# An S5 drive two half units earlier in a hybrid decoder trunk: VectorE's branch work, scores and S5 outputs in another order

## The reference

```
h    = x * (1 + scale) + shift
proj = h @ w_in                       # 2048 -> 6144, in 12 parts of 512 channels
A: y_a = a_b * causal_conv3(a_c * a_x) * silu(a_g)
B: y_b = dilated window attention(q, k, v), 8 heads of 64, three dilations mixed * silu(b_g)
C: y_c = RG-LRU(causal_conv4(c_x)) * silu(c_g)      # two gate products, one scan over time
D: y_d = S5(d_u) * silu(d_g)          # complex diagonal scan, y = Re(C x) + D u, gelu, GLU
y    = concat(y_a, y_b, y_c, y_d) @ w_out
x    = LayerNorm(alpha * x + (1 + gate) * y)
```

## Time and profile before

| | |
|---|---|
| median of three runs | 1848.13 us (1841.9 to 1850.42) |
| profiled execution, its own time | 1842.14 us |
| span of its profile | 1840.3 us |
| mean granted TensorE clock | 0.957 of full speed |
| TensorE busy (matmuls) | 1669.3 us, 91% |
| VectorE busy | 1249.6 us, 68% |
| ScalarE busy | 774.4 us, 42% |
| POOL busy | 233.1 us, 13% |

### The profile page before, as it was taken

How to read it: one execution, slowest core, us unless ns; L and a number is a source line. 1 busy time by engine, 2 the same in 40 slices (tenths; PEclk the granted TensorE clock), 3 DMA queues, 4 the chain that set the end, 5 groups by cost and what they waited for, 6 DMA issues and landing times.

```text
span 1840.3 us, 23052 instructions
## 1 busy us (share of the span) xinstructions
PE 1669.3 (91%) x7527; PEld 1294.5 (70%) x7527; DVE 1249.6 (68%) x2361; ACT 774.4 (42%) x1014; POOL 233.1 (13%) x281
## 2 busy tenths in 40 slices
PE   2339999999999999799998999999999999979995
PEld 1337778777777877568876777777877777748884
DVE  5885984895698489556673587398378468643658
ACT  2135444554544454421226554554555455432220
POOL 2242111111111111000004111111111111100000
PEclk9559999999999999899998999999999999989998
DMA  7999879978988988747656888978988887727422
GB/s 261 375 328 255 216 188 234 237 197 217 231 204 207 244 211 208 194 148 236 199 183 187 191 192 196 218 186 196 203 201 200 186 203 190 183 80 257 137 92 103
DMA packets 322945, 376.07 MB, mean 204 GB/s; under 512 B 27064, under 2 KB 224032, under 8 KB 319784
## 3 DMA queue, kind: packets, MB, share of 16 engines
q1 hardware_dynamic: 294632, 272.36, 46.0%
q0 software_dynamic: 28224, 102.77, 31.0%
HBM read 261.81 MB, written 10.51 MB: 148 GB/s over the span
## 4 chain that ended last, share of the span: by engine, by line
PE 58%; DVE 30%; issue 6%; DMA 3%; ACT 1%; SPq 1%; DVEq 0%; POOL 0%; ACTq 0%; POOLq 0%
PE bank L944 12%; PE bank L951 11%; PE bank L945 11%; DVE work L1285 9%; PE bank L987 6%; PE bank L984 6%; PE bank L985 6%; DVE ada_acc L1293 3%; DVE work L1293 3%; DVE work L1147 2%; DVE work L1146 2%; PE bank L963 2%; DVE carry L1293 2%; DVE y_t L1293 1%; DVE work L1289 1%
## 5 line engine op out<-in xcount | busy, mean ns | idle before, releaser
L944 PE MATMUL bank<-op_hi,w_hi 128*128 128x512 f32 x1536 | 617.5, 402 | 0.0
L945 PE MATMUL bank<-op_lo,w_hi 128*128 128x512 f32 x1536 | 602.8, 392 | 0.0
L951 PE MATMUL bank<-op_hi,w_lo 128*128 128x512 f32 x1536 | 379.9, 389 | 4.3 <-DMA w_lo<-raw 4.3
L598 ACT ACTIVATE w_hi<-raw 128x1024 fp32r<-128x1024 f32 x196 | 207.8, 1060 | 397.7 <-PE bank L945 315.1
L944 PEld LDWEIGHTS bank<-op_hi,w_hi 128*128 128x128 f32 x1536 | 290.7, 189 | 88.6 <-issue 21.3
L951 PEld LDWEIGHTS bank<-op_hi,w_lo 128*128 128x128 f32 x1536 | 288.0, 188 | 65.5 <-DMA w_lo<-raw 5.8
L945 PEld LDWEIGHTS bank<-op_lo,w_hi 128*128 128x128 f32 x1536 | 290.7, 189 | 60.1 <-issue 1.9
L550 POOL DMA_DIRECT2D w_lo<-raw x196 | 170.7, 871 | 1077.5 <-ACT w_lo L601 1058.4
L601 ACT ACTIVATE w_lo<-raw 128x1024 fp32r<-128x1024 f32 x196 | 207.2, 1057 | 111.6 <-PE bank L951 111.6
L1293 DVE SCALAR_TENSOR_TENSOR ada_acc<-ada_in,cond,ada_acc 128x512 f32<-128x512 f32 (+1 forms) x234 | 181.4, 775 | 82.3 <-DMA ada_in<-in_w_ada 60.8
L984 PE MATMUL bank<-w_hi,op_hi 128*128 128x512 f32 x480 | 188.2, 392 | 0.0
(11 more groups left out here) (226 smaller groups left out, 1600.8 us busy)
## 6 DMA issues: line engine op xcount, KB each, us to landing
w_lo<-raw POOLq DMA_DIRECT2D x196, 512.0 KB, 5.0
raw<-in_w_in SPq DMA_DIRECT2D x192, 512.0 KB, 4.3
ada_in<-in_w_ada SPq DMA_DIRECT2D x256, 256.0 KB, 4.5
raw<-in_w_out SPq DMA_DIRECT2D x64, 512.0 KB, 4.2
raw<-in_w_ada SPq DMA_DIRECT2D x27, 512.0 KB, 7.0
ada_in<-in_w_ada SPq DMA_DIRECT2D x18, 512.0 KB, 7.1
rot<-in_w_ada SPq DMA_DIRECT2D x10, 512.0 KB, 7.0
bias_t<-in_w_ada SPq DMA_DIRECT2D x9, 512.0 KB, 7.0
```

The source lines that it names most:

```text
L598: act.activation(w_hi[:, n % NHL, :], raw[:, n % NRAW, :], ACT.Copy).then_inc(s.hi_done.sem, 1)
L944: pe.matmul(o, w_hi[:, n % NHL, w], op_hi[:, k, :], start=k == 0, stop=False)
L945: mm = pe.matmul(o, w_hi[:, n % NHL, w], op_lo[:, k, :], start=False, stop=False)
L951: mm = pe.matmul(o, w_lo[:, n % NHL, w], op_hi[:, k, :], start=False, stop=k == KT - 1)
```

## The change

It reorders work and adds or removes none. On TensorE `s5_turn` goes from behind half unit 3 to behind 2, the drives from 5, 7, 10, 13 to 3, 5, 8, 12, `s5_outputs` from 19 to 18, and `scores(2)` and `scores(3)` from 12, 13 to 11, 12. On ScalarE `rotation()` is done behind `split_hi(4)` instead of behind the copy of c_x at 5. On VectorE the LRU's conv goes behind `s5_in(0)`, `s5_in(1)` ahead of the LRU, the score maxima behind later S5 work, `s5_in(3)` ahead of `normalise`, the pieces' calls 11 and 12 elsewhere, and A's conv ahead of D's output. SyncE's and POOL's programs are the same.

```diff
@@ -684,10 +684,11 @@
                             for h in range(2):
                                 swapped = act.activation(u_swap[64 * h:64 * h + 64, :], ps[64 - 64 * h:128 - 64 * h, :], ACT.Copy)
                             swapped.then_inc(free.sem, 1)
+                        if n == 4:
+                            rotation()
                         if n == 5:
                             act.wait_ge(s.step_end.sem, s.step_end.at(0, ct))
                             copy("c_x", xp[:, 3:3 + S])
-                            rotation()
                         if n == 7:
                             copy("q", q_t, HD ** -0.5)
                         if n == 8:
@@ -918,12 +919,12 @@
                     def put(n, part, *args):
                         between[n].append(lambda: part(*args))
 
-                    put(3, s5_turn)
+                    put(2, s5_turn)
                     put(6, lru_gates)
-                    for q, at in enumerate((5, 7, 10, 13)):
+                    for q, at in enumerate((3, 5, 8, 12)):
                         put(at, s5_drive, q)
-                    put(19, s5_outputs)
-                    for t, at in enumerate((9, 10, 12, 13)):
+                    put(18, s5_outputs)
+                    for t, at in enumerate((9, 10, 11, 12)):
                         put(at, scores, t)
                     put(11, v_turn)
                     for g, (at_turn, at_weigh) in enumerate(((16, 18), (18, 20), (20, 22))):
@@ -1107,13 +1108,6 @@
                 ada(2, 1)
                 ada(2, 1)
 
-                unit_copied(dve, s, "c_x", ct)
-                own(ts(xc, xp[:, 3:3 + S], col("conv_c", 12), MUL, col("conv_c_b"), ADD), s.own)
-                for k in (2, 1):
-                    own(stt(xc, xp[:, k:k + S], col("conv_c", 4 * k), xc, MUL, ADD), s.own)
-                own(stt(xc, xp[:, 0:S], col("conv_c"), xc, MUL, ADD), s.xc_done)
-                ada(2, 1)
-
                 w_re, w_im, t_ = (v.rearrange("p (a b) -> p a b", a=4) for v in s5_s[0:3])
                 states = state_tiles(ct)
 
@@ -1193,10 +1187,17 @@
 
                 dve.wait_ge(x_io.sem, 16 * (1 + (ST if l else 0)))
                 s5_in(0)
+                unit_copied(dve, s, "c_x", ct)
+                own(ts(xc, xp[:, 3:3 + S], col("conv_c", 12), MUL, col("conv_c_b"), ADD), s.own)
+                for k in (2, 1):
+                    own(stt(xc, xp[:, k:k + S], col("conv_c", 4 * k), xc, MUL, ADD), s.own)
+                own(stt(xc, xp[:, 0:S], col("conv_c"), xc, MUL, ADD), s.xc_done)
+                ada(2, 1)
                 s5_scan(0)
                 ada(2, 1)
                 s5_out(0)
                 ada(2, 1)
+                s5_in(1)
 
                 dve.wait_ge(s.from_act.sem, s.from_act.at(2, ct))
                 own(ts(lru_s[0], lru_s[0], 1.0, ADD), s.own)
@@ -1207,30 +1208,38 @@
                 own(tt(lru_s[1], lru_s[1], lru_s[2], MUL), s.own)
                 own(dve.tensor_tensor_scan(xc, lru_s[0], lru_s[1], 0.0, MUL, ADD), s.own)
                 ada(2, 1)
-                score_max(0)
-                s5_in(1)
                 s5_scan(1)
                 ada(2, 1)
-                score_max(1)
+                score_max(0)
                 s5_out(1)
                 ada(2, 1)
-                score_max(2)
+                score_max(1)
                 s5_in(2)
                 ada(2, 1)
+                score_max(2)
+                s5_scan(2)
                 score_max(3)
-                s5_scan(2)
+                s5_out(2)
                 ada(2, 1)
-                s5_out(2)
+                s5_in(3)
+                ada(2, 1)
                 normalise(0)
-                ada(2, 1)
                 normalise(1)
                 own(silu2(0, "c_g", gx[:, 0, :]), s.own)
                 own(stt(y_out(2), xc, 0.5, gx[:, 0, :], MUL, MUL), s.gate_used[0])
-                s5_in(3)
+                ada(2, 1)
                 s5_scan(3)
-                ada(2, 1)
                 s5_out(3)
                 own(silu2(1, "d_g", silu_d[:, bass.ds(ct, 1), :].rearrange("p o t -> p (o t)")), s.gate_used[1])
+                ada(2, 1)
+
+                unit_copied(dve, s, "a_x", ct)
+                v = va[:, 2:2 + S]
+                own(tt(v, v, ax, MUL), s.own)
+                cv = s5_s[1]
+                own(ts(cv, v, col("conv_a", 8), MUL), s.own)
+                own(stt(cv, va[:, 1:1 + S], col("conv_a", 4), cv, MUL, ADD), s.own)
+                own(stt(cv, va[:, 0:S], col("conv_a"), cv, MUL, ADD), s.own)
                 ada(2, 1)
 
                 y = s5_s[0]
@@ -1241,15 +1250,6 @@
                 own(tt(gel, s5_s[2], y, MUL), s.to_act)
                 ada(2, 1)
 
-                unit_copied(dve, s, "a_x", ct)
-                v = va[:, 2:2 + S]
-                own(tt(v, v, ax, MUL), s.own)
-                cv = s5_s[1]
-                own(ts(cv, v, col("conv_a", 8), MUL), s.own)
-                own(stt(cv, va[:, 1:1 + S], col("conv_a", 4), cv, MUL, ADD), s.own)
-                own(stt(cv, va[:, 0:S], col("conv_a"), cv, MUL, ADD), s.own)
-
-                ada(2, 1)
                 own(silu2(0, "b_g", gx[:, 0, :]), s.own)
                 dve.wait_ge(s.pv_done.sem, s.pv_done.at(2 * ST, ct))
                 own(stt(y_out(1), bank[7][:, :], 0.5, gx[:, 0, :], MUL, MUL), s.free[7])
```

More of the change, by code:

```diff
@@ L1228, in branch_loop @@
                 own(stt(y_out(2), xc, 0.5, gx[:, 0, :], MUL, MUL), s.gate_used[0])
-                s5_in(3)
+                ada(2, 1)
                 s5_scan(3)
-                ada(2, 1)
                 s5_out(3)
                 own(silu2(1, "d_g", silu_d[:, bass.ds(ct, 1), :].rearrange("p o t -> p (o t)")), s.gate_used[1])
-                ada(2, 1)
-                y = s5_s[0]
-                dve.wait_ge(s.c_done.sem, s.c_done.at(SQ, ct))
-                own(stt(y, u_d, col("s5_d"), bank[4][:, :], MUL, ADD), s.free[4])
-                own(tt(s5_s[2], y, y, MUL), s.own)
-                own(ts(s5_s[2], s5_s[2], 0.044715, MUL, 1.0, ADD), s.own)
-                own(tt(gel, s5_s[2], y, MUL), s.to_act)
                 ada(2, 1)
@@ L1250, in branch_loop @@
                 own(stt(cv, va[:, 0:S], col("conv_a"), cv, MUL, ADD), s.own)
+                ada(2, 1)
+                y = s5_s[0]
+                dve.wait_ge(s.c_done.sem, s.c_done.at(SQ, ct))
+                own(stt(y, u_d, col("s5_d"), bank[4][:, :], MUL, ADD), s.free[4])
+                own(tt(s5_s[2], y, y, MUL), s.own)
+                own(ts(s5_s[2], s5_s[2], 0.044715, MUL, 1.0, ADD), s.own)
+                own(tt(gel, s5_s[2], y, MUL), s.to_act)
                 ada(2, 1)
```

## The result

The changed kernel takes **1884.14 us** (median of four runs, 1882.96 to 1887.32), the kernel before in the same batch 1849.28 (four runs, 1841.9 to 1853.04). The ratio is **1.0215**, 95% interval 1.0192 to 1.0237: slower by 35 us. The forecast was 1878, slower by 1.6%, with a range of 1848 to 1897.

The account below looks back on a forecast made before the run. Neither TensorE (58% of the chain) nor VectorE (30%) alone was the bound. Layer 1 12.8, layer 0 11 and clock 6.4, together +30 on 1842.14, gave 1872; the median lies 6 higher: 1878 us, range 1848 to 1897.

Parts of the forecast that it names:

- 1, the head start: Start of VectorE's long run: `s5_in(0)` at 23.5 us of the step instead of 34.6, net 6 to 7 earlier.
- 8: Items priced at nothing: ScalarE's rotation, POOL's loads, SyncE's pairs, A's conv; wait at the turn of the probabilities gone, or almost.
- 2, the scores in layer 0: Later first score maximum: TensorE waits 3.2 us at `scores(1)`, 0.6 to 0.7 more at `scores(2)`; no wait in layer 1.
- 3 to 6, the load: Ahead of the fourth scan VectorE waits for call 12's load; TensorE then waits at `s5_outputs`, 4.7 us (layer 1), 4.6 (layer 0).
- rival B: Call 12 does not wait for its load; VectorE's own work sets layer 0's `s5_out(3)`: 1845 us, chance 0.12.
- 7, the clock: TensorE's lower clock behind the outputs' waits: 0 to 1.6 or 1.7 us each, half taken, 0.8 a step, 6.4 in all.
- C: VectorE's head start carries through, decided at `scores(1)` after half unit 10, and all waits go: 1819 us, chance 0.06.

Follow-up runs that it names:

- last experiment: Changed kernel with outputs at 19, last drive at 13, score maxima earlier, `s5_in(3)` behind `normalise` and C's output, call 12 behind the fourth scan: 1816.49 us, ratio 0.985.

## Why the prediction was right, and which term was too small

**1, the head start: right.** `s5_in(0)` starts at 23.8 of the step, 23.5 was forecast. **8, right:** the wait at the turn of the probabilities is gone in all eight steps, and no step shows the rotation's cost.

**2, the scores in layer 0: right, less its second wait.** 3.5 us of wait a step, and none in layer 1. The forecast was 3.2 and 0.6 to 0.7 for the next one, which did not appear. The outputs-at-19 run shows this term alone: its layer 0 step is 5.0 us above the 151.83 of the last experiment, of which 3.5 are the wait and 1.5 what followed it.

**3 to 6, the load: right in mechanism and size.** The second pass of half unit 16 in layer 1 was forecast at 102.3 of the step and began at 102.4; the landing was taken at 5.7 and was 5.3; the end of `s5_out(3)` was put at 120.8 and the instruction behind it began at 120.7; the wait at the outputs was to be 4.7 and was 4.5. In layer 0 it was to be 4.6 and was 5.6: the first load went out at 108.5 of the step instead of 107.1 (the clock behind the scores' wait had held TensorE up), and issuing it took SyncE 1.5 us instead of 0.88. Some 1.9 of these 5.6 stay without that load, by the run with the piece behind the scan: VectorE's own work, which the prediction had in rival B alone, at 2.7. The sum of both kinds of wait over the eight steps: forecast 4 x (3.9 + 4.6) + 4 x 4.7 = 52.8 us, measured 14.1 + 39.3 = 53.4. Three experiments take the load's part away in three ways (the piece behind the scan, the load sooner, the consumer later), and each removes the wait in step 1 of layer 1, or all but 0.4 of it.

**7, the clock: the mis-sized term.** The prediction took "half, 0.8 a step", 6.4 in all, between nothing and 1.6 or 1.7 a wait. It went wrong in three ways. It priced only the eight waits at the outputs and put nothing on the four at the scores. It took half of the price where each wait paid most of it or all: all twelve waits of the changed kernel have a low clock behind them. And at the outputs in layer 1 the price lay above its upper bound, at 2.2. (Its row for the longest wait was misread besides: the wait ahead of 1624.80 was 8.6 us, not 7.9.) From the outputs in layer 0, timeline of TensorE:

```profile
429.23 1.06 PE L843 MATMUL bank<-y_t,s_w 128*32 x1 [5.64 <-DVE work L1285]
...
430.08 1.06 PE L843 MATMUL bank<-y_t,s_w 128*32 x1
```

A group of four matmuls starts every 0.85 us here. In the run with the outputs at 19, in a step of layer 1, where nothing waited ahead of them, it was 0.43:

```profile
1279.70 0.59 PE L843 MATMUL bank<-y_t,s_w 128*32 x1
...
1280.13 0.59 PE L843 MATMUL bank<-y_t,s_w 128*32 x1
```

The former is TensorE at the lower of its two levels, 1.2 instead of 2.4 GHz. In layer 1 the price is the 157.17 of the step less the 150.45 of the run without a wait less the wait of 4.5: 2.2 us. In layer 0, 163.85 less 151.83 less 9.2 of waits: 2.8 for two, of which 1.5 go to the wait of 3.5 at the scores by the outputs-at-19 run. That leaves 1.3 for the 5.6 at the outputs: the longer wait did not cost more. The clock rows in the result section say the same: 0.70 over 5.4 us behind that wait loses 1.6 us, 0.58 in layer 1 loses 2.3. So 4 x 2.8 + 4 x 2.2 = 20 us by this reckoning, some of which the kernel before already paid: two of its waits had a low clock behind them, and a wait costs a little more than its length even at full clock (157.20 less 151.83 less 5.1 of waits leaves 0.3 for three). Between the two traces the loop of layer 0 is 24.1 us longer and that of layer 1 20.1, together 44.2 (from the first matmul of each to the last); the waits named above grew by 53.4 - 25.0 = 28.4; so 15.8 us are left for the clock and the drained pipeline (0.6 of them longer waits for weights), where the prediction had 6.4 for the clock. Before the GLU of layer 0 1.8 us come back, since TensorE's wait for the GLU's weights is that much shorter. 28.4 + 15.8 - 1.8 = 42.4 of the 42.9 between the profiled executions.

The rule of the Trainium skill that the prediction weighed (TensorE: Matmul & The Clock Gate, "What's actually happening": throttled is the default that activity releases) would have had all eight waits at the outputs pay, 12.8 instead of 6.4. That was the better choice for these waits: all of them did. Taken of every wait, whatever its length, it would not agree with these traces, as the last section shows.

**The medians.** The forecast stood 6 us above the profiled execution of before, because the median did; after's own median is 0.9 below its profiled execution. So the nearness of 1878 to 1884.14 is in part luck: a sum of +30 was forecast, +42.9 was measured between the traces, and +35 between the medians. The median of 1849.28 rests on four runs; the 25 and 19 runs of the later batches gave 1844.92 and 1845.51, and against those the changed kernel would be some 39 us slower.

**The rivals.** B, that call 12 would not wait, is what the run with the piece behind the scan makes true: 1845.16, where B had 1845, though made up otherwise: its layer 1 steps are at 150.45 and those of layer 0 at 159.4 to 159.8, where B had 158.1, for the scores' wait and its clock. C, faster by the head start, has a kernel too, the last one above: 1816.49, where C had 1819 with all waits gone. The place that C named as decisive, `scores(1)` behind half unit 10, was one of the two.

## What to carry to other kernels

An in-order engine that is started earlier gains only as far as the next thing it waits for: look through its whole list for the first point where it will now be ahead of a producer (here a load whose issue hangs on a buffer released by TensorE, and scores not yet computed), and move the work behind that point, or give the consumer one more unit of slack. Two edits, a piece ahead of a scan and a consumer one unit sooner, cost 2% together, and either one put back takes the loss away. In a kernel bound by TensorE, price a new wait at its length plus what the clock loses behind it, here another 1.3 to 2.2 us for waits of 3.5 to 5.6, and not more for the longer one.

## What the runs showed of the hardware

**The clock behind a wait.** In the branch loops of the two kernels and the seven experiments, from 250 us on and without the waits for weights, the granted clock over the 5.4 us behind a wait of TensorE was 0.50 to 0.71 after each of the 22 waits of 3.39 us and longer. Behind the 45 waits of 0.8 to 2.8 us it was full 31 times and low 14 times (two of the low ones, waits of 0.8, have another wait of 2.5 in the same 5.4 us), and waits of one length were found with either: 2.78 us with 1.00 and with 0.68 in the same kernel at the same place of different steps, 1.7 us with 0.68, 0.71 and 1.00. One wait of 3.21 us had 1.00 behind it. So length makes it likely and does not alone decide it; what else does is open.

**A wait of 1.7 us may cost twice its length.** In the run with the early maxima the layer 1 step was 154.11 with one wait of 1.7, against 150.71 without it in the run with the outputs at 19: 3.4 us.

**Landings.** The 256 KB loads of call 12 took 4.4 to 6.0 us to land in the eight steps of the changed kernel, and up to 8.0 us in the run with the load sooner, where two stood behind two bias tiles, beside a weight load issued some 3 us later that took 10.6.
